# RMS norms of a 512-token block stack: reciprocal root on four columns, spread to rows by TensorE

## The chip, the cores and the metric

The kernel runs on one core of one Trainium2 chip. The metric is the device time of one execution in microseconds. The kernel before took 4485.65 us (median of 3 runs, 4485.53 to 4496.6).

## The reference

Two stacks of transformer blocks work on 512 tokens of width 1024 in fp32. The first has four layers with a mixer (hyena, window attention, pooling, hyena) and a SwiGLU each; the second has one layer with a gated delta rule, latent attention, a merge and an MLP. Ahead of every mixer and every feed-forward stands a root mean square norm:

```python
def rmsnorm(x, g):
    xf = x.astype(jnp.float32)
    y = xf * lax.rsqrt(jnp.mean(xf * xf, axis=-1, keepdims=True) + EPS)
    return (y * g.astype(jnp.float32)).astype(x.dtype)

def _modulate(xn, shift, scale):
    return xn * (1.0 + scale) + shift

# first stack, layer i
h = rmsnorm(x, norm_mix[i]);  x = x + mixer(h)
x = x + swiglu(rmsnorm(x, norm_ffn[i]), ff_w_gate[i], ff_w_up[i], ff_w_down[i])
# second stack
h  = _modulate(_rms(x, norm_attn[l]), mod_x[0], mod_x[1])
hc = _modulate(_rms(ctx, norm_attn[l]), mod_c[0], mod_c[1])
x  = x + mod_x[5] * _sq_relu_mlp(_modulate(_rms(x, norm_mlp[l]), mod_x[3], mod_x[4]), ...)
```

That makes eight norms in the first stack and, in the second, two over the 512 tokens and one over the 256 tokens of the context.

## The kernel before, in words

The activations `x` lie transposed in SBUF: 128 partitions (features) by 8 tiles (`DT`) by 512 tokens (`T`). A sum over the features of a token is therefore a sum over partitions and tiles. Weights come from HBM through a ring of blocks that SyncE loads. Most products (L880 to L882, L891 to L893) are made of three products of rounded high and low parts: ScalarE copies the high part of a weight block (L1748, L1760), GpSimd subtracts it from the block to get the low part (L774, L798), and each product of a 128x128 weight tile with a 128x512 activation tile is three matmuls. PSUM has eight banks: four `acc` banks take the products in rotation and four `aux` banks everything else. Every tile of a rotation is numbered; TensorE waits on `aux_drained[...]` before it writes a bank for the fifth time, and readers wait on `aux_full`.

The order on each engine is that of one list of stages. All synchronisation is by semaphores, and each engine works its queue in order.

A norm goes as follows. ScalarE squares each of the eight tiles of `x` into `xn` (L1764, L1781), VectorE adds squares 1 to 6 onto square 0 (`fold`, L2336), most of it while the stage before still runs. When the last addition is done, TensorE multiplies a 128x128 matrix of ones with the folded tile (L867) and with tile 7 (L870) into one bank. That sums over the partitions and leaves the sum of every token in every partition, as 128x512. Each fp32 matmul is two records in the trace. ScalarE meanwhile loads the table with the square root and makes a dummy root (L1789), then takes the root of the bank into `rstd` (128x512, L1791):

```python
signal(go(rstd, bank(t, aux=True)[:], ACT.Sqrt, bias=eps_col, scale=1.0 / D), root_set)
```

VectorE inverts it in place (L2322 in a norm, L2626 in `modulate`), which also gives the bank free, and makes the eight normed tiles, each a multiplication by the gain of its features and by `rstd` (L2327, L2628):

```python
signal(stt(xn[:, k, :], x[:, k, :], V(gain[0], gain[1] + k), rstd, ALU.mult, ALU.mult),
```

Ahead of a feed-forward or a hyena mixer, ScalarE copies each normed tile to a rounded high part (L1755), VectorE subtracts to get the low part (L2307) and the first products (L891 to L893) run tile by tile as these arrive. Ahead of attention, TensorE waits for all eight tiles (L859). Ahead of pooling, VectorE goes on by itself (L2568 and on). In `modulate` VectorE adds a shift to every tile (L2629). In the first of the two `modulate` stages the norm of the context follows (L1196, L2006, L2641, L2643), in the old form in both kernels. Behind the first norm stands a small product for the attention bias (L1703), and behind a hyena norm the first sine layer (L939).

Elsewhere the kernel has the other form already. The sums over features of q and k heads are columns (L1072, L1281, L1416, L1543: the data is the stationary operand, one column of ones the moving one), their root (L2133) and reciprocal (L2884) are taken on a few columns, and TensorE spreads a column to rows (L1423) with a broadcast column as the stationary operand and the unit matrix as the moving one.

Of the kernel before, what the change touches and what calls it, by code (L numbers as in the profile page):

```python
# [14 lines left out]
P = 128  # L15
T = 512
TC = 256
D = 1024
# [261 lines left out]
def build_program(nc, stream, vecs, tabs, tabs2, x_in, ctx_in, first_mods, scratch, x_keep, diag, solved_t, solved_n, out, schedule):  # L280
# [4 lines left out]
    with ExitStack() as stack:  # L285
# [3 lines left out]
        def sem(name):  # L289
            return stack.enter_context(nc.semaphore(name))  # L290
# [57 lines left out]
        one_col = small_t[:, 7:8]  # L348

# [45 lines left out]
        folded_set = sem("folded_set")  # L395
        root_set = sem("root_set")
# [156 lines left out]
        def _(sp):  # L553
# [43 lines left out]
            def norm(_):  # L597
                n["aux"] += 1
                n["xn"] += DT
# [34 lines left out]
            def modulate(which):  # L634
                n["aux"] += 1 if which else 2
# [78 lines left out]
        def _(pool):  # L714
# [101 lines left out]
            def passes(aux, acc):  # L816
                def stage(_):
# [5 lines left out]
            run({"norm": count(1), "hyena": hyena,  # L823
                 "attention": passes(12 + 16 * 5, 88), "pool": passes(0, DT), "ffn": split("ffn", FT + 2 * DT), "mod": nothing,
                 "modulate": lambda which: n.update(aux=n["aux"] + (1 if which else 2)), "decays": count(2),
# [5 lines left out]
        def _(pe):  # L831
# [31 lines left out]
            def norm(gain):  # L863
                b = open_aux()
                n["fold"] += 1
                pe.wait_ge(folded_set, n["fold"])
                mm(b[:], ones[:], xn[:, 0, :], start=True, stop=False)  # L867
                n["sq"] += DT
                pe.wait_ge(squares_set, n["sq"])
                mm(b[:], ones[:], xn[:, DT - 1, :], start=False, stop=True).then_inc(aux_full, 1)  # L870
                n["xn"] += DT
# [838 lines left out]
        def _(act):  # L1710
# [61 lines left out]
            def norm(gain, then=None):  # L1772
# [17 lines left out]
                t = full(aux, aux_full)  # L1790
                signal(go(rstd, bank(t, aux=True)[:], ACT.Sqrt, bias=eps_col, scale=1.0 / D), root_set)  # L1791
# [482 lines left out]
        def _(dve):  # L2274
# [40 lines left out]
            def norm(gain):  # L2315
                if n["root"] == 0:
                    for k in range(1, DT - 1):
                        fold(k)
                t = aux.take()
                n["root"] += 1  # L2320
                dve.wait_ge(root_set, n["root"])
                drain(nc.vector.reciprocal(rstd, rstd), t, True)  # L2322
                n["xn"] += DT
                target = split_target(gain)
                to = (x_hi_h, xn_r) if target == "hyena" else (x_hi, x_lo)
                for k in range(DT):
                    signal(stt(xn[:, k, :], x[:, k, :], V(gain[0], gain[1] + k), rstd, ALU.mult, ALU.mult),  # L2327
                           plain_set if target else xn_set)
                    if target and k:
                        low(k - 1, *to)  # L2330
                if target:
                    low(DT - 1, *to)

            def fold(k):
                dve.wait_ge(squares_set, n["sq"] + k + 1)
                ins = tt_(xn[:, 0, :], xn[:, 0, :], xn[:, k, :], ALU.add)  # L2336
                if k < DT - 2:
                    step(ins)
                else:
                    signal(ins, folded_set)  # L2340
                    n["sq"] += DT

# [273 lines left out]
            def modulate(which):  # L2616
# [6 lines left out]
                t = aux.take()  # L2623
                n["root"] += 1
                dve.wait_ge(root_set, n["root"])
                drain(nc.vector.reciprocal(rstd, rstd), t, True)  # L2626
                for k in range(DT):
                    step(stt(xn[:, k, :], x[:, k, :], gm[:, 0, k:k + 1], rstd, ALU.mult, ALU.mult))  # L2628
                    signal(ts_(xn[:, k, :], xn[:, k, :], modv[:, shift + k, 0:1], None, ALU.add), plain_set if which else xn_set)  # L2629
                    if which and k:  # L2630
                        low(k - 1)
                if which:
                    low(DT - 1)
# [663 lines left out]
```

## Time and profile before

| | |
|---|---|
| median of 3 runs | 4485.65 us |
| the profiled execution | 4489.94 us |
| its span in the trace | 4488.1 us |
| PE busy | 4152.2 us, 93% |
| DVE busy | 2123.1 us, 47% |
| ACT busy | 1223.2 us, 27% |
| GpSimd busy | 1444.5 us, 32% |
| mean granted TensorE clock | 0.956 of full |

The profiled execution took 1.8 us more than its span, and 4.3 us more than the median of the runs. Times in the views below are microseconds from the start of the span. The granted clock of TensorE has two levels in this trace, 1.00 (2.4 GHz) and 0.50 (1.2 GHz). A fp32 matmul appears as two records of a weight load (PEld) and two of a matmul (PE).

### The profile page before, as it was taken

The numbers are of one execution on the slowest core, as the hardware profiler recorded it, in microseconds if no ns is written. First come the engines' busy times: TensorE is split into PE (matmuls) and PEld (weight loads), VectorE is DVE, ScalarE is ACT, GpSimd is POOL, SyncE is SP. The second block draws the span as 40 slices with busy tenths as digits, with TensorE's granted clock in tenths as the row PEclk, the third lists the DMA queues.
The fourth block names the chain that finished last, engine by engine and source line by source line (L and its number), as shares of the span: only waits on it lengthen the run. The fifth ranks groups of instructions, "written<-read, shape, count | busy, mean of one in ns | idle before, by whom it ended". The sixth has DMA issues, their size and how long they took to land.

```text
span 4488.1 us, 47580 instructions
## 1 busy us (share of the span) xinstructions
PE 4152.2 (93%) x18926; PEld 3071.3 (68%) x18926; DVE 2123.1 (47%) x3109; ACT 1223.2 (27%) x1709; POOL 1444.5 (32%) x834
## 2 busy tenths in 40 slices
PE   7999999899999599989999998979998999998999
PEld 5656788556788378877557886656666665684887
DVE  6567323365413641375763334456664347404322
ACT  3322222134222121233233222322222224422221
POOL 3311344200344144434023442266564000241443
PEclk9999999999999899999999998989999879999999
DMA  6200232210232123221002221221112112221232
GB/s 179 75 18 21 110 102 88 104 47 29 98 114 83 61 97 115 82 78 63 29 29 103 98 95 60 69 57 33 56 34 57 58 67 66 68 98 64 86 104 78
DMA packets 96910, 333.71 MB, mean 74 GB/s; under 512 B 44337, under 2 KB 47537, under 8 KB 67889
## 3 DMA queue, kind: packets, MB, share of 16 engines
q1 hardware_dynamic: 87968, 311.85, 20.5%
q10 hardware_dynamic: 8720, 18.82, 1.7%
q8 instruction: 151, 2.47, 0.2%
q14 instruction: 71, 0.57, 0.0%
HBM read 317.53 MB, written 13.11 MB: 74 GB/s over the span
## 4 chain that ended last, share of the span: by engine, by line
PE 79%; DVE 14%; POOL 2%; ACT 2%; issue 1%; DMA 1%; SPq 0%; DVEq 0%; ACTq 0%; POOLq 0%
PE bank L880 16%; PE bank L881 16%; PE bank L882 16%; PE bank L1314 5%; PE bank L859 5%; PE bank L1082 3%; PE bank L1032 1%; PE bank L1056 1%; PE bank L1612 1%; PE bank L1611 1%; PE bank L1633 1%; PE bank L1543 1%; DVE xn L2327 1%; POOL tab L761 1%; POOL tab L759 1%
## 5 line engine op out<-in xcount | busy, mean ns | idle before, releaser
L774 POOL TENSOR_TENSOR w_lo<-ring,w_hi 128x2048 fp32r<-128x2048 f32 (+2 forms) x200 | 775.3, 3877 | 1532.7 <-ACT w_hi L1748 1532.7
L880 PE MATMUL bank<-x_hi,w_hi 128*128 128x512 f32 x1584 | 618.3, 390 | 9.7 <-POOL w_lo L774 9.7
L881 PE MATMUL bank<-x_lo,w_hi 128*128 128x512 f32 x1584 | 617.0, 389 | 0.0
L882 PE MATMUL bank<-x_hi,w_lo 128*128 128x512 f32 x1584 | 616.9, 389 | 0.0
L1748 ACT ACTIVATE w_hi<-ring 128x2048 fp32r<-128x2048 f32 (+2 forms) x200 | 322.0, 1610 | 866.9 <-PE bank L882 865.9
L880 PE MATMUL bank<-h_hi,w_hi 128*128 128x512 f32 x960 | 373.9, 389 | 0.4
L881 PE MATMUL bank<-h_lo,w_hi 128*128 128x512 f32 x960 | 373.5, 389 | 0.0
L882 PE MATMUL bank<-h_hi,w_lo 128*128 128x512 f32 x960 | 373.4, 389 | 0.0
L880 PEld LDWEIGHTS bank<-x_hi,w_hi 128*128 128x128 f32 x1584 | 297.7, 188 | 73.4 <-POOL w_lo L774 11.8
L882 PEld LDWEIGHTS bank<-x_hi,w_lo 128*128 128x128 f32 x1584 | 297.8, 188 | 61.9
L881 PEld LDWEIGHTS bank<-x_lo,w_hi 128*128 128x128 f32 x1584 | 297.8, 188 | 61.6
L2363 DVE TENSOR_TENSOR xn<-bank,xn 128x512 f32<-128x512 f32 x88 | 60.8, 691 | 589.0 <-PE bank L882 570.0
L1314 PE MATMUL bank<-xn,ring 128*128 128x512 f32 x496 | 240.0, 621 | 1.4 <-DVE work L2671 1.4
L1082 PE MATMUL bank<-work,tab 128*128 128x512 f32 x512 | 228.0, 603 | 12.5 <-ACT work L1886 11.5
L787 POOL TENSOR_TENSOR ring_r<-ring,merge_hi 128x2048 fp32r<-128x2048 f32 x16 | 73.3, 4584 | 506.8 <-ACT merge_hi L2213 506.8
L2353 DVE TENSOR_TENSOR x<-bank,x 128x512 f32<-128x512 f32 x72 | 49.8, 692 | 393.8 <-PE bank L882 347.3
L880 PEld LDWEIGHTS bank<-h_hi,w_hi 128*128 128x128 f32 x960 | 180.2, 188 | 39.3 <-DVE h_lo L2313 2.1
L882 PEld LDWEIGHTS bank<-h_hi,w_lo 128*128 128x128 f32 x960 | 180.2, 188 | 37.4
L881 PEld LDWEIGHTS bank<-h_lo,w_hi 128*128 128x128 f32 x960 | 180.2, 188 | 37.3
L1082 PEld LDWEIGHTS bank<-work,tab 128*128 128x128 f32 x512 | 97.8, 193 | 133.4 <-issue 126.9
L810 POOL TENSOR_TENSOR work<-work,ring 128x1024 f32<-128x1024 f32 x32 | 77.0, 2429 | 266.4 <-ACT work L1855 266.4
L761 POOL TENSOR_TENSOR tab<-tab 56x31 f32<-56x31 f32 (+15 forms) x248 | 150.7, 608 | 19.4
(457 smaller groups left out, 7394.4 us busy)
## 6 DMA issues: line engine op xcount, KB each, us to landing
ring<-stream SPq DMA_DIRECT2D x212, 1024.0 KB, 4.8
ring<-stream SPq DMA_DIRECT2D x64, 704.0 KB, 4.1
ring<-stream SPq DMA_DIRECT2D x36, 512.0 KB, 3.6
xn<-first_mods SPq DMA_DIRECT2D x8, 1024.0 KB, 6.9
ring<-stream SPq DMA_DIRECT2D x4, 1088.0 KB, 5.0
bias_rows<-work ACTq DMA_DIRECT2D x1, 4096.0 KB, 46.3
work<-bias_rows ACTq DMA_DIRECT2D x1, 3072.0 KB, 11.3
tab<-tabs ACTq DMA_DIRECT2D x1, 2624.0 KB, 16.7
```

The costliest lines, as they stand in the source:

```text
L761: solve(tt(W[:, 0:i, i:SUB], W[:, 0:i, i:SUB], part, ALU.subtract))
L774: nc.gpsimd.tensor_tensor(w_lo[:, j % 2, 0:cols], ring[:, k % RING, 0:cols], w_hi[:, j % 2, 0:cols], ALU.subtract).then_inc(wlo_set, 1)
L787: nc.gpsimd.tensor_tensor(ring_r[:, w, 0:2 * DT * P], ring[:, w, 0:2 * DT * P], merge_whi[j % 2][:], ALU.subtract).then_inc(wlo_set, 1)
L810: nc.gpsimd.tensor_tensor(pair, pair, decay[:, pq:pq + 1, :].broadcast_to([P, 2, 512]), ALU.mult).then_inc(filt_set, 1)
L859: ins = mm(b[:], w[:, at + k, :], rhs[k] if isinstance(rhs, list) else rhs[:, k, :], start=(k == 0), stop=(k == kt - 1))
L880: mm(b[:], hi[:, at + k, :], rhs_hi, start=(k == 0), stop=False)
L881: mm(b[:], hi[:, at + k, :], rhs_lo[:, k, :], start=False, stop=False)
L882: ins = mm(b[:], lo[:, at + k, :], rhs_hi, start=False, stop=(k == kt - 1))
L1082: ins = mm(b[:], fwd[kind][:, p, q, ft * P:(ft + 1) * P], source(kind)[:, 2 * p + q, :], start=(q == 0), stop=(q == 1))
L1314: ins = mm(b[:, 0:TC] if ctx else b[:], w[:, at + k, :], src[:, k, :], start=(k == 0), stop=(k == DT - 1))
L1748: signal(go(w_hi[:, j % 2, 0:cols], ring[:, k % RING, 0:cols], ACT.Copy), whi_set)
L2363: drain(tt_(h_tmp[:, f % 2, :], bank(t)[:], gate_tmp[:, f % 2, :], ALU.mult), t)
```

## The change

Ten norms change: the eight `norm` stages and the two norms over 512 tokens of `modulate`. The sum of a token becomes one element of a column: for each chunk of 128 tokens the folded tile is the stationary operand and one column of ones the moving one; the same is done for tile 7 into four more columns. VectorE copies the first four columns to `rstd_col` (128x4) and adds the other four. ScalarE takes the root and VectorE the reciprocal on these 128x4. TensorE then spreads the four columns to a 128x512 bank, and the normed tiles read this bank instead of `rstd`. The bank is given free, by a one-column memset of VectorE, after the eighth normed tile. A norm takes two `aux` tiles instead of one, and the counts of every engine follow. The norm of the context stays.

```diff
@@ PE, norm
-                mm(b[:], ones[:], xn[:, 0, :], start=True, stop=False)
+                for c in range(NB):
+                    mm(b[:, c:c + 1], xn[:, 0, P * c:P * (c + 1)], ones[:, 0:1], start=True, stop=True)
                 n["sq"] += DT
                 pe.wait_ge(squares_set, n["sq"])
-                mm(b[:], ones[:], xn[:, DT - 1, :], start=False, stop=True).then_inc(aux_full, 1)
+                for c in range(NB):
+                    ins = mm(b[:, NB + c:NB + c + 1], xn[:, DT - 1, P * c:P * (c + 1)], ones[:, 0:1], start=True, stop=True)
+                ins.then_inc(aux_full, 1)
+                b = open_aux()
+                pe.wait_ge(rstd_set, n["fold"])
+                for c in range(NB):
+                    ins = mm(b[:, P * c:P * (c + 1)], rstd_col[:, c:c + 1].broadcast_to([P, P]), ident[:], start=True, stop=True)
+                ins.then_inc(aux_full, 1)
@@ ACT, norm
-                t = full(aux, aux_full)
-                signal(go(rstd, bank(t, aux=True)[:], ACT.Sqrt, bias=eps_col, scale=1.0 / D), root_set)
+                t = aux.take()
+                aux.take()
+                act.wait_ge(aux_drained[aux.place(t)], aux.turn(t) + 1)
+                signal(go(rstd_col, rstd_col, ACT.Sqrt, bias=eps_col, scale=1.0 / D), root_set)
@@ DVE, norm (modulate likewise)
-                t = aux.take()
-                n["root"] += 1
-                dve.wait_ge(root_set, n["root"])
-                drain(nc.vector.reciprocal(rstd, rstd), t, True)
+                t, rows = rstd_rows()
...
-                    signal(stt(xn[:, k, :], x[:, k, :], V(gain[0], gain[1] + k), rstd, ALU.mult, ALU.mult),
+                    signal(stt(xn[:, k, :], x[:, k, :], V(gain[0], gain[1] + k), rows, ALU.mult, ALU.mult),
                            plain_set if target else xn_set)
                     if target and k:
                         low(k - 1, *to)
+                rows_read(t)
                 if target:
                     low(DT - 1, *to)
@@ DVE, new
+            def rstd_rows():
+                t = full(aux, aux_full)
+                b = bank(t, True)
+                step(nc.vector.tensor_copy(rstd_col, b[:, 0:NB]))
+                ins = tt_(rstd_col, b[:, NB:2 * NB], rstd_col, ALU.add)
+                drain(ins, t, True)
+                n["root"] += 1
+                dve.wait_ge(root_set, n["root"])
+                signal(nc.vector.reciprocal(rstd_col, rstd_col), rstd_set)
+                t = full(aux, aux_full)
+                return t, bank(t, True)[:]
+
+            def rows_read(t):
+                which = aux_drained[t % BANKS]
+                nc.vector.memset(small_t[:, 25:26], 0.0).then_inc(which, 1)
+                dve.wait_ge(which, t // BANKS + 1)
```

## Rows read from the trace of the kernel before

**Rows 1.** The page: busy time (share of span) and instructions; the chain by engine.
```profile
PE 4152.2 (93%) x18926; PEld 3071.3 (68%) x18926; DVE 2123.1 (47%) x3109; ACT 1223.2 (27%) x1709; POOL 1444.5 (32%) x834
...
PE 79%; DVE 14%; POOL 2%; ACT 2%; issue 1%; DMA 1%; SPq 0%; DVEq 0%; ACTq 0%; POOLq 0%
```

**Rows 2.** The chain in order of time, around one norm: start, length, what.
```profile
472.98 0.70 DVE xn L2336
473.81 1.10 PE bank L867 x2
474.91 0.87 PE bank L870 x2
475.87 0.70 ACT rstd_t L1791
476.66 3.37 DVE rstd_t L2322
480.05 0.76 DVE xn L2327
...
482.46 0.77 PE bank L891
```

**Rows 3.** VectorE's instructions on `rstd_t`: duration ns min/median/max, first and last start.
```profile
L2327 DVE SCALAR_TENSOR_TENSOR xn<-x,vec,rstd_t x64: 750/752/3577, 23.7 to 2411.7; 128x512 f32<-128x512 f32 x64
...
L2322 DVE RECIPROCAL rstd_t<-rstd_t x8: 3352/3354/3355, 20.3 to 2398.5; 128x512 f32<-128x512 f32 x8
...
L2626 DVE RECIPROCAL rstd_t<-rstd_t x2: 3352/3352/3353, 2781.2 to 4108.5; 128x512 f32<-128x512 f32 x2
```

**Rows 4.** Timeline from 195: column sums at full clock and their reader.
```profile
194.86 3.63 PE L1072 MATMUL bank<-ones,work 128*128 128x1 f32 x32
...
198.62 0.18 DVE L2420 RECIPROCAL small_t<-bank 128x4 f32<-128x4 f32 x1 [2.22 <-PE bank L1072]
```

**Rows 5.** Timeline from 3506: column sums, root, reciprocal, spread, reader of the bank.
```profile
3506.43 1.16 PE L1423 MATMUL bank<-ident,tab 128*128 128x128 f32 x8 [0.15 <-DVE tab L2884]
...
3510.19 1.22 PE L1416 MATMUL bank<-ones,work 128*128 128x1 f32 x8 [1.71 <-ACT work L2078]
3511.51 0.27 ACT L2133 ACTIVATE tab<-bank,small_t 128x4 f32<-128x4 f32 x1 [1.46 <-PE bank L1416]
3511.88 0.18 DVE L2884 RECIPROCAL tab<-tab 128x4 f32<-128x4 f32 x1 [1.04 <-ACT tab L2133]
...
3512.11 2.07 PE L1423 MATMUL bank<-ident,tab 128*128 128x128 f32 x8 [0.70 <-DVE tab L2884]
3514.29 0.75 DVE L2901 SCALAR_TENSOR_TENSOR work<-work,vec,bank 128x512 f32<-128x512 f32 x1 [2.23 <-PE bank L1423]
```

**Rows 6.** Stretches: length, PE, PEld, DVE, ACT, POOL busy, granted clock, DMA.
```profile
475.77:482.46 6.69, 0.00 (x0) 0.03 (x1) 5.66 (x5) 1.95 (x3) 0.00 (x0) 0.80 0.07 29
482.46:486.67 4.21, 4.21 (x10) 3.34 (x11) 4.04 (x6) 1.72 (x3) 0.00 (x0) 0.50 0.00 0
...
3616.70:3620.10 3.40, 3.40 (x33) 3.40 (x32) 0.00 (x0) 0.00 (x0) 0.00 (x0) 1.00 0.95 393
3620.10:3623.50 3.40, 3.40 (x13) 2.87 (x14) 0.61 (x3) 0.22 (x1) 0.00 (x0) 0.50 0.49 205
```

**Rows 7.** Timeline from 3446: column sums at half clock.
```profile
3446.05 2.70 PE L1281 MATMUL bank<-tab,work 128*128 128x1 f32 x12
```

**Rows 8.** Timeline of the first norm: GpSimd's subtraction and the normed tiles.
```profile
22.19 4.50 POOL L798 TENSOR_TENSOR ring_r<-ring,z_lo 128x2048 fp32r<-128x2048 f32 x1 [20.57 <-ACT z_lo L1760]
23.66 4.36 DVE L2327 SCALAR_TENSOR_TENSOR xn<-x,vec,rstd_t 128x512 f32<-128x512 f32 x2
```

**Rows 9.** Timeline of the first `modulate`: last fold and first normed tile.
```profile
2775.71 0.69 DVE L2336 TENSOR_TENSOR xn<-xn 128x512 f32<-128x512 f32 x1 [7.52 <-ACT xn L1764]
...
2784.57 0.75 DVE L2628 SCALAR_TENSOR_TENSOR xn<-x,gm,rstd_t 128x512 f32<-128x512 f32 x1
```

**Rows 10.** The page's costliest groups: an addition that reads a bank.
```profile
L2353 DVE TENSOR_TENSOR x<-bank,x 128x512 f32<-128x512 f32 x72 | 49.8, 692 | 393.8 <-PE bank L882 347.3
```

More of the change, by code:

```diff
@@ L348, in build_program @@
         one_col = small_t[:, 7:8]
+        rstd_col = small_t[:, 28:32]
         def carve(*sizes):
@@ L395, in build_program @@
         folded_set = sem("folded_set")
+        rstd_set = sem("rstd_set")
         root_set = sem("root_set")
@@ L597, in norm @@
             def norm(_):
-                n["aux"] += 1
+                n["aux"] += 2
                 n["xn"] += DT
@@ L634, in modulate @@
             def modulate(which):
-                n["aux"] += 1 if which else 2
+                n["aux"] += 2 if which else 3
             def decays(_):
@@ L822, in _ @@
             nothing = count(0)
-            run({"norm": count(1), "hyena": hyena,
+            run({"norm": count(2), "hyena": hyena,
                  "attention": passes(12 + 16 * 5, 88), "pool": passes(0, DT), "ffn": split("ffn", FT + 2 * DT), "mod": nothing,
-                 "modulate": lambda which: n.update(aux=n["aux"] + (1 if which else 2)), "decays": count(2),
+                 "modulate": lambda which: n.update(aux=n["aux"] + (2 if which else 3)), "decays": count(2),
                  "gdn": gdn, "mla": nothing, "merge": merge,
@@ L2622, in modulate @@
                     step(tt_(gm[:, c, :], gm[:, c, :], gain, ALU.mult))
[L2623 to L2626, printed above, removed]
+                t, rows = rstd_rows()
                 for k in range(DT):
-                    step(stt(xn[:, k, :], x[:, k, :], gm[:, 0, k:k + 1], rstd, ALU.mult, ALU.mult))
+                    step(stt(xn[:, k, :], x[:, k, :], gm[:, 0, k:k + 1], rows, ALU.mult, ALU.mult))
                     signal(ts_(xn[:, k, :], xn[:, k, :], modv[:, shift + k, 0:1], None, ALU.add), plain_set if which else xn_set)
@@ L2631, in modulate @@
                         low(k - 1)
+                rows_read(t)
                 if which:
```

## The prediction

> **What bounds the kernel now.** I read the page's busy times and its chain first: TensorE is busy 93% of the span and carries 79% of the chain, VectorE 14% [rows 1]. So the kernel is a stream of matmuls, and what a norm costs is the time in which that stream stands still. The chain in order of time shows it for the norm behind the first hyena mixer [rows 2]: the last fold ends at 473.68 (472.98 + 0.70), the sums run from 473.81, the root from 475.87, the reciprocal from 476.66 and the first normed tile from 480.05; the first product starts at 482.46. From the end of the fold to the first normed tile it is 6.37 us, and more than half of it is the 128x512 reciprocal, 3.37 us. Everything in this stretch is on the chain; TensorE does nothing from 475.77 to 482.46 [rows 6]. The same reciprocal stands in all ten norms, x8 and x2, each 3352 to 3355 ns [rows 3]. I read the other norms' timelines too: eight of the ten have this pattern within 0.02 us. The two others are the first norm, which runs beside a GpSimd subtraction [rows 8], and the first `modulate`, which starts at half clock and takes 8.17 us from the end of the fold (2775.71 + 0.69 = 2776.40) to the first tile at 2784.57 [rows 9].
>
> The change therefore touches ten stretches of the chain, about 66 us together, 1.5% of the time, and nothing else of weight.
>
> **The change part by part, for one of the eight.**
>
> - Fold to sums: 473.68 to 473.81, 0.13 us, stays [rows 2].
> - Column sums. Before, four records of 512 columns, from 473.81 until the root starts at 475.87: 2.06 us. Now there are 8 fp32 matmuls of one column, 16 records, each behind its own weight load. At full clock 32 such records take 3.63 us (0.113 each), and their reader starts 3.76 us after the first [rows 4]; 16 of them then take 3.76 - 16 x 0.113 = 1.95 us. At half clock 12 take 2.70 us, 0.225 each [rows 7]; 16 take 3.60 us and, with the 0.13 us to the reader, 3.73 us. These are the ends.
> - Copy and addition on 128x4: new. The nearest row is a 128x4 operation of VectorE that reads a bank, 0.18 us [rows 4]; two of them, 0.03 us between them and 0.06 us to ScalarE make 0.45 us.
> - Root on 128x4 instead of 128x512: 3511.51 to 3511.88, 0.37 us with the hand-over to VectorE, where the row before had 0.79 us (475.87 to 476.66) [rows 5, 2].
> - Reciprocal on 128x4: 3511.88 to 3512.11, 0.23 us with the hand-over to TensorE, where 3.39 us stood (476.66 to 480.05) [rows 5, 2].
> - The spread: four fp32 matmuls, 8 records of 128 columns. The kernel has just this elsewhere: 2.07 us at half clock, its reader starting 2.18 us after the first record, and 1.16 us at full clock, which with the same 0.11 us gives 1.27 us [rows 5].
>
> With everything at full clock the chain is 0.13 + 1.95 + 0.45 + 0.37 + 0.23 + 1.27 = 4.40 us, 1.97 less than now. With everything at half clock it is 0.13 + 3.73 + 0.45 + 0.37 + 0.23 + 2.18 = 7.09 us, 0.72 more than now. So the reciprocal's 3.1 us are there to be had, and the clock decides how many of them TensorE takes back.
>
> What the trace says of the clock: in 3616.70 to 3620.10 TensorE is busy the whole time with one-column sums (33 records) at 1.00, and in the next stretch it runs at 0.50 (1.2 GHz) [rows 6]. The sums in rows 7 run at 0.50 behind a like train. And the spread at 3506.43 takes 1.16 us while the one at 3512.11, behind 8 one-column sums (1.22 us), takes 2.07 us [rows 5]. So the clock falls behind one-column sums in which TensorE counts as busy. Before, the two 512-column sums run at full clock, TensorE then idles 6.69 us, over which the mean clock is 0.80, and the first ten records of product run at 0.50 for 4.21 us [rows 6]. After the change the wide sums are gone, and the last wide work is the products of the stage before. I expect the fall within the few us behind that: about as often in the column sums as behind them, and nearly always before the spread, which starts some 3.5 us after the fold. I take 2.4 us for the sums (between 1.95 and 3.73; nearer to the full-clock row, as the fall, where it comes in them, leaves only their second part slow) and 2.18 us for the spread (the half-clock row). That gives 0.13 + 2.4 + 0.45 + 0.37 + 0.23 + 2.18 = 5.76 us, 0.61 less than now. Eight norms: 4.9 us.
>
> The half-clock stretch of the products behind stays: they still start 2.41 us behind the first tile (480.05 to 482.46), with TensorE idle before them [rows 2]. It starts earlier by what the norm saves, no more.
>
> - First `modulate`: it starts at half clock, so 8.17 us become 7.09: 1.1 us saved. The context sums queued behind the spread on TensorE move back some 2 us; their reader, ScalarE's second root, waits for the last normed tile more than 9 us later, which hides it.
> - First norm: also at half clock. The first normed tile starts 7.09 us behind the fold's end at 15.70, at 22.79 instead of 23.66. There is a second thing. That tile should take 0.75 us, but the first two take 4.36 us together while GpSimd's subtraction runs from 22.19 to 26.69 [rows 8], and the largest of the 64 is 3577 ns against a median of 752 [rows 3]. So VectorE's operation with two SBUF inputs was held until GpSimd was done. With the rows in a bank it has one SBUF input. I take it to go through; but the subtraction for the low part of tile 0 (two SBUF inputs) is held in its place, to about 27.35 (GpSimd's end, 0.1 later than before, and the 0.55 us that the held one took behind it), where it ended at 28.75 before. Saved: 1.4 us. If the tile is held as before, it is nothing to 0.9.
> - The memset that frees the bank: VectorE's small operation and its wait, 0.1 us, in front of the last low part. Seven times it hides behind TensorE, which is late there after its half-clock stretch; ahead of pooling it is on the chain. I take 0.1 us in all, at most 1.
> - Waits added: ScalarE waits for VectorE's addition instead of for TensorE. Behind it stand the copies of high parts, which need normed tiles anyhow. TensorE waits for the reciprocal; behind it stand the bias product and the sine layer (about 1 us each), which fit in the 5 us before the first product. No DMA and no SyncE step moves; the second `aux` tile per norm is free long before its bank comes round.
>
> Sum: 4.9 + 1.1 + 1.4 - 0.1 = 7.3 us. The profiled execution would go from 4489.94 to 4482.6 us. It lies 4.3 us above the median of the runs; from the median 4485.65 I get 4478.
>
> A page speaks against the multiplications. The Trainium skill, "VectorE: DVE Perf Modes", section "The TRN2 errata — SBUF-src ops pay a fixed extra latency per instruction", gives VectorE a fixed term of 120 cycles with a PSUM source and 58 with SBUF, at 0.96 GHz 65 ns more; over 80 normed tiles an estimate of 5.2 us by that page, and 4483 instead of 4478. The trace disagrees: a multiplication that reads a bank takes 0.75 us [rows 5] against 752 ns from SBUF [rows 3], and an addition 692 ns from a bank [rows 10] against 0.69 [rows 9]. I count nothing.
>
> A page bears on the first norm: the Trainium skill, "SBUF — State Buffer", section "SBUF: two separate sides", says that a VectorE operation with two SBUF inputs contends with a GpSimd operation that reads SBUF, and the later one waits for the other's end. By that rule the bank input goes through (1.4 us), without it 0.9 at most; rows 8 agree with it as far as the old form goes.
>
> **The rivals.**
>
> - *The clock holds through sums and spread.* 1.97 x 8 = 15.8 us, with 2.4 us of the two others 18 us: 4467. For it: the fall has been seen only behind trains of one-column sums, and here they are short. Against: rows 5, where eight of them sufficed. If the clock also held into the products, up to 4.21 - 10 x 0.23 = 1.9 us more in seven norms, 4455.
> - *The other side: the clock falls ahead of the sums.* If losing the wide sums lets it fall before the column sums begin, each of the eight costs 0.72 us more than now: +5.8 - 1.1 - 1.4 + 0.1 = +3.4, 4489. It decides where the sums take more than 2.4 + 7.3 / 8 = 3.3 us on average. For it: half clock at the start of the first `modulate`, behind 9 us of idling. Against: the gap here is under 2 us behind dense products, and the wide sums before started at full clock.
> - *Reading the bank is dearer than SBUF*: the 4483 above on the page's terms; from rows, 0.
>
> **How the numbers follow.** Forecast 0.56, clock holds 0.15 (and into the products 0.05), clock falls early 0.18, the dearer bank or something else 0.06. About 0.3% (13.5 us) is what a measurement of this kernel can tell from no change; the forecast's 7.3 us lie within it. The forecast's own range is 4472 to 4484; the range to 4463 and 4491 takes in the two neighbouring cases. Faster by over 0.3% (below 4472.2): 0.2 from the two cases with the held clock and 0.02 of the forecast's edge. Slower by over 0.3% (above 4499.1): no case reaches it, 0.04 for what I have not seen. Within: 0.74.
>
> **What would show it.** The reciprocals fall from 33.5 us to about 2. Column sums between 1.9 and 3.8 us per norm, differing from norm to norm by where the clock falls; spreads mostly at 2.07 and seldom at 1.16. First normed tile about 5.8 us behind the fold's end instead of 6.37. No 3577 ns tile in the first norm. I am wrong if spreads at full clock are the rule, if the fall comes before the sums, or if normed tiles take clearly over 0.75 us.

## The result, and the profile after

The changed kernel takes 4497.35 us (median of 20 runs, 4489.35 to 4501.64), the kernel before took 4488.61 in the same session (20 runs, 4479.96 to 4499.58). The ratio is 1.0018, 95% interval 1.0011 to 1.0025: the change costs 5 to 11 us where I forecast a gain of 7, and 4497.35 lies above the range given (4463 to 4491). The profiled execution took 4501.48 us (span 4499.7), against 4489.94 before.

The page after; the lines answer to [rows 1]:
```profile
PE 4197.2 (93%) x19126; PEld 3120.5 (69%) x19126; DVE 2100.6 (47%) x3139; ACT 1219.3 (27%) x1709; POOL 1444.8 (32%) x834
...
PE 79%; DVE 13%; POOL 3%; ACT 2%; issue 2%; DMA 1%; SPq 0%; DVEq 0%; ACTq 0%; POOLq 0%
```
VectorE has lost 22.5 us of work, which is what was wanted. TensorE is busy 45 us longer with 200 more matmuls. The norms explain the 200 records (ten times 16 + 8 - 4), but only 22 of the 45 us (their sums and spreads keep TensorE busy for 44.7 us in all, the wide sums did for 22.9); the rest must be old matmuls that got slower.

The norm behind the first hyena mixer, where [rows 2] stood. Chain in order of time: start, length, what.
```profile
477.71 0.70 DVE xn L2346
...
478.55 1.02 PE bank L870 x8
479.58 0.91 PE bank L874 x8
...
480.57 0.17 DVE small_t L2356
480.77 0.17 DVE small_t L2357
...
481.03 0.30 ACT small_t L1803
...
481.42 0.19 DVE small_t L2361
...
481.75 2.06 PE bank L879 x8
...
483.90 0.76 DVE xn L2336
...
486.32 0.76 PE bank L901
```
From the fold's end (478.41) to the first normed tile it is 5.49 us instead of 6.37, and from there to the first product (486.32) 2.42, as before (2.41). So the norm itself is 0.88 us shorter. The same stretches by busy time, granted clock in the eighth column, as in [rows 6]:
```profile
478.55:480.98 2.43, 1.92 (x16) 1.83 (x16) 0.32 (x2) 1.36 (x2) 0.00 (x0) 1.00 0.89 378
480.99:481.75 0.76, 0.00 (x1) 0.03 (x1) 0.18 (x1) 0.30 (x1) 0.00 (x0) 0.50 0.01 0
481.75:483.81 2.06, 2.05 (x8) 1.75 (x8) 0.00 (x0) 0.00 (x0) 0.00 (x0) 0.50 0.00 0
...
486.32:491.23 4.91, 4.91 (x12) 3.84 (x13) 4.70 (x7) 1.89 (x3) 0.00 (x0) 0.50 0.01 3
491.23:495.00 3.77, 3.77 (x18) 3.13 (x17) 3.60 (x6) 1.68 (x3) 0.00 (x0) 1.00 0.00 0
```
The clock falls at 480.98, 2.57 us behind the fold (before it fell 6.17 us behind it in this norm, and 4.4 to 6.6 us in the eight norms that lie alike), so the spread runs at half clock. And the products now spend 4.91 us at half clock, where they spent 4.21.

The small operations, answering to [rows 3]: duration in ns, min/median/max.
```profile
L2356 DVE COPY small_t<-bank x10: 160/161/163, 19.8 to 4119.1; 128x4 f32<-128x4 f32 x10
L2357 DVE TENSOR_TENSOR small_t<-bank,small_t x10: 160/161/163, 20.0 to 4119.3; 128x4 f32<-128x4 f32 x10
L2361 DVE RECIPROCAL small_t<-small_t x10: 177/178/179, 20.6 to 4119.9; 128x4 f32<-128x4 f32 x10
```
The normed tiles that read the bank:
```profile
L2336 DVE SCALAR_TENSOR_TENSOR xn<-x,vec,bank x64: 746/748/749, 23.1 to 2422.4; 128x512 f32<-128x512 f32 x64
```
No tile of 3577 ns is left. The spread, by its records:
```profile
L879 PE MATMUL bank<-ident,small_t x80: 421/421/580, 20.9 to 4121.9; 128*128 128x128 f32 x80
```
All 80 have a half-clock duration (at full clock eight of them take 1.16 us in all [rows 5]). The timeline of the first norm, where [rows 8] stood:
```profile
22.55 4.51 POOL L800 TENSOR_TENSOR ring_r<-ring,z_lo 128x2048 fp32r<-128x2048 f32 x1 [20.93 <-ACT z_lo L1770]
...
23.05 1.53 DVE L2336 SCALAR_TENSOR_TENSOR xn<-x,vec,bank 128x512 f32<-128x512 f32 x2 [2.24 <-PE bank L879]
...
24.63 2.98 DVE L2319 TENSOR_TENSOR xn_r<-xn,x_hi_h 128x512 fp32r<-128x512 f32 x1
```
Two normed tiles now go through beside GpSimd, and the next operation with two SBUF inputs is held to 27.61, GpSimd's end and 0.55 us, in their place.

**Norm by norm.** From the fold's end to the first normed tile, before and after: 6.38 and 5.50 us in five norms (three of the four ahead of an ffn, the one ahead of the second hyena mixer, the second `modulate`), 6.38 and 5.70 in two (ahead of attention and of pooling), 6.38 and 6.81 in one (ahead of the ffn behind pooling), 8.17 and 7.13 in the first `modulate`, 7.96 and 7.07 in the first norm. Together 7.3 us saved. All this is one execution: in a second trace of the same kernel (the first experiment) nine of the ten norms are within 0.1 us of this, and the norm ahead of the ffn behind pooling takes 5.06 us instead of 6.81.

**Where the time went.** I cut both traces at the ends of the folds and compare the stages, each with the norm at its head:

| stage | before us | after us | after less before |
|---|---|---|---|
| first hyena mixer | 457.97 | 462.42 | +4.45 |
| ffn 0 | 373.49 | 372.93 | -0.56 |
| attention | 282.42 | 282.37 | -0.05 |
| ffn 1 | 373.25 | 373.00 | -0.25 |
| pooling | 66.07 | 66.07 | 0.00 |
| ffn 2 | 376.24 | 376.66 | +0.42 |
| second hyena mixer | 450.32 | 457.59 | +7.27 |
| ffn 3 | 380.94 | 380.52 | -0.42 |
| second stack | 1329.10 | 1329.39 | +0.29 |
| last mlp | 382.64 | 382.76 | +0.12 |

Two readings. No stage gets all that its norm saves: pooling gets none of 0.68, attention 0.05 of 0.68, ffn 0, 1 and 3 get 0.25 to 0.56 of 0.88, the last mlp none. And one stage, the second hyena mixer, loses 7.3 us although its norm saves 0.88. (The first hyena mixer's stage differs from one execution of the same kernel to the next by more than that, 452.9 to 462.4 in two of the changed kernel; I set it aside.) Behind the first product of the second hyena mixer, first before and then after: the stretch from the first product to the rise of the clock, the whole stage behind it, and 30 us in its middle (not quite the same work: 112 matmul records and 99).
```profile
1953.93:1957.81 3.88, 3.87 (x9) 3.14 (x10) 3.71 (x6) 1.38 (x3) 0.00 (x0) 0.50 0.00 0
1953.93:2395.47 441.54, 412.64 (x1540) 283.36 (x1540) 297.97 (x336) 135.58 (x170) 117.55 (x33) 0.96 0.14 48
2163.00:2193.00 30.00, 28.09 (x112) 18.38 (x112) 17.03 (x21) 9.00 (x15) 7.32 (x4) 0.94 0.00 1
```
```profile
1957.33:1962.37 5.04, 5.04 (x12) 3.97 (x13) 4.83 (x7) 1.89 (x3) 0.00 (x0) 0.50 0.00 0
1957.33:2407.01 449.68, 421.30 (x1540) 289.70 (x1540) 300.06 (x337) 135.57 (x170) 117.61 (x33) 0.95 0.13 47
2169.00:2199.00 30.00, 29.65 (x99) 19.06 (x100) 15.97 (x20) 6.84 (x12) 5.07 (x3) 0.83 0.00 1
```
The same 1540 matmuls, the same work on ScalarE and GpSimd, but TensorE busy 8.7 us longer and the stage 8.14 us longer. Counting through the stage with its norm, TensorE stands at half clock for 34.1 us before and 54.6 after, and half of the 20.5 us between them is 10, near the 8 that are lost: the products did not change, the clock falls under them more often. Aligning the 1540 records of the two traces one by one, the distance between them grows by 8.7 us inside stretches that are at half clock in one of the traces, and shrinks by 0.6 us outside them.

### The profile page after: what moved, and what is told of

It reads as the page before. It is cut to its first block, busy times and chain, and to the rows that moved or that the text cites. A ratio compares the mean times of both kernels' runs of the same rounds, so it can differ in the third digit from the quotient of the medians.

```text
span 4499.7 us, 48040 instructions
## 1 busy us (share of the span) xinstructions
PE 4197.2 (93%) x19126; PEld 3120.5 (69%) x19126; DVE 2100.6 (47%) x3139; ACT 1219.3 (27%) x1709; POOL 1444.8 (32%) x834
## 4 chain that ended last, share of the span: by engine, by line
PE 79%; DVE 13%; POOL 3%; ACT 2%; issue 2%; DMA 1%; SPq 0%; DVEq 0%; ACTq 0%; POOLq 0%
PE bank L890 16%; PE bank L891 16%; PE bank L892 16%; PE bank L1324 5%; PE bank L861 5%; PE bank L1092 3%; PE bank L1042 2%; PE bank L1066 2%; PE bank L1622 1%; PE bank L1621 1%; PE bank L1643 1%; PE bank L1553 1%; POOL tab L763 1%; DVE xn L2336 1%; POOL tab L761 1%
## 5 line engine op out<-in xcount | busy, mean ns | idle before, releaser
L1042 PE MATMUL bank<-tab,work 128*128 128x256 f32 x512 | 128.3, 414 | 30.8 <-DVE work L2524 30.8
```

The costliest lines, as they stand in the source:

```text
L1042: ins = mm(b[:, 256 * p:256 * (p + 1)], U[:, 4 * ft + 2 * kind + p, ct * P:(ct + 1) * P], inv[kind][:, p, ft, :], start=(j == 0), stop=(j ...
```

## The experiments

The theory: the half-clock stretch behind a norm ends at an instant that the clock sets and not the kernel. Work of fixed length follows, so each norm fixes how the stage behind it lies to the clock's further instants. The change moves that, and the second hyena mixer meets them badly. (The expectations below call this the phase theory: the phase is where the work lies between two such instants.) The main rivals: the added bank turns, the column sums or the narrow root as such cost time further on; the difference is scatter; the fall ahead of the spread is the whole loss. Ratios are to the kernel before on the same chip, with 95% intervals, and times are medians.

**The changed kernel again** (no edit).

> The changed kernel once more, for a second trace. Phase theory (the instants at which the clock falls stand in a fixed relation to the work, because each stretch at half clock ends at such an instant and the work behind it is of fixed length): the falls behind the feed-forward norms come again 2.5 to 2.7 us behind the end of the fold, as in five norms of the first trace, and the hyena stages again hold clearly more than the 34 us at half clock that the second hyena stage of the kernel before had. Chance theory (each execution draws its own phase): both numbers scatter by more than 1 us from norm to norm and execution to execution, and the hyena stages are as often short as long. Time 4492 to 4502 us by both.

4497.17 us, ratio 1.0012 (1.0002 to 1.0023); profiled execution 4492.14. The first hyena mixer's stage is 452.89 here, and from there to the end it is 4021.5 us, as in the first trace (4021.3), against 4014.4 before. The second hyena mixer's stage is 457.64 again, so its 7.3 us are the kernel's, not scatter. The falls ahead of ffn 0, 1 and 3 come 2.5 to 2.8 us behind the fold, about as the phase theory has it. The one ahead of the ffn behind pooling does not come again: it stood 0.49 us behind the fold in the first trace and stands 3.83 us behind it here, within the spread, whose eight records take 1.61 us, between the 1.16 of full and the 2.05 of half clock:
```profile
1566.72 1.61 PE L879 MATMUL bank<-ident,small_t 128*128 128x128 f32 x8 [1.28 <-DVE small_t L2361]
```
That norm is 1.75 us shorter than in the first trace, 5.06 instead of 6.81, and its stage is 376.54 instead of 376.66. One kernel thus shows by itself that what a norm saves can be gone by the end of its stage.

**The old arithmetic on the new banks.** Wide sums, root and reciprocal as before; two `aux` tiles a norm, the second filled by a single one-column matmul and freed by the memset.
```diff
-                for c in range(NB):
-                    mm(b[:, c:c + 1], xn[:, 0, P * c:P * (c + 1)], ones[:, 0:1], start=True, stop=True)
+                mm(b[:], ones[:], xn[:, 0, :], start=True, stop=False)
...
                 b = open_aux()
-                pe.wait_ge(rstd_set, n["fold"])
-                for c in range(NB):
-                    ins = mm(b[:, P * c:P * (c + 1)], rstd_col[:, c:c + 1].broadcast_to([P, P]), ident[:], start=True, stop=True)
-                ins.then_inc(aux_full, 1)
+                mm(b[:, 0:1], ones[:], ones[:, 0:1], start=True, stop=True).then_inc(aux_full, 1)
```

> The sums, root and reciprocal on 128x512 as before, but two aux tiles per norm, the second written by a one-column matmul and freed by the memset: the bank rotation, the waits and the memset of the change alone. Bank theory (the shifted rotation makes waits in the hyena stages): the hyena stages lose their 5 to 8 us each here too, 4498 to 4506 us. Phase theory: nothing moves by more than 0.1 us in a norm, so the time is that of the kernel before, within 3 us. Column theory (what costs is that the wide sums are gone): also that of the kernel before.

4490.85 us, 1.0003 (0.9992 to 1.0013). The second hyena mixer's stage is 450.30, behind the first product 441.51: the kernel before's. Bank turns, memsets and their waits are cleared. Further on this trace shows what does scatter: the second stack takes 1325.17 us where the kernel before had 1329.10, the last mlp 381.00 where it had 382.64. Differences of up to 4 us in the second stack are therefore not read as effects here.

**Delays in the two hyena norms.** Memsets of the now unused `rstd_t` ahead of the small reciprocal, two and then four of them; one took 0.65 us.
```diff
+                for _ in range(delay):
+                    step(nc.vector.memset(rstd_t[:], 0.0))
                 signal(nc.vector.reciprocal(rstd_col, rstd_col), rstd_set)
```

> The changed kernel with two VectorE memsets of 128x512 (about 1.0 us together) ahead of the small reciprocal in the two norms before hyena mixers only. Phase theory: the hyena stages meet the clock's instants elsewhere, and the time moves by much more or by another sign than the 2 us put in: at least 4 us away from the changed kernel plus 2 here or in the 2 us variant. Bank theory and every theory by which an instruction or a wait costs: the changed kernel plus 2 us, within 1.5.

> The same with four memsets (about 2.1 us). Phase theory: as in the 1 us variant; of the two, one is expected to have stretches at half clock as few as in the kernel before (34 us in a hyena stage), and to be faster than the changed kernel in spite of the delay. Theories of cost: the changed kernel plus 4 us, within 1.5.

Two memsets: 4484.59 us, 0.9985 (0.9973 to 0.9998). Four: 4484.82, 0.9993 (0.9982 to 1.0003), an interval that takes in no difference from the kernel before. Both medians lie 12 us below the changed kernel's 4497.17 on the same chip. In both the first normed tile comes later by the memsets' 1.3 and 2.6 us, and the second hyena mixer's stage is shorter all the same: 450.88 and 447.82, where the changed kernel had 457.6. Added work on the chain that shortens its stage by 6.7 and 9.8 us is what the theory says and no rival does.

**One memset, in the norm ahead of the second hyena mixer alone.**
```diff
+                t, rows = rstd_rows(1 if gain == ("norm_mix", 3 * DT) else 0)
```

> The changed kernel with one VectorE memset (0.65 us in the chain, as measured in the delayed kernels) in the norm ahead of the second hyena mixer only. Phase theory: the distance from the stage's first product to the rise of the clock behind it is 5.04 us in the changed kernel (stage behind the first product 449.7 us), 3.88 in the kernel before (441.5) and 4.10 with 1.3 us of delay (441.7). Here it becomes about 4.4, on the side of the good ones: 442 us behind the first product if the step lies above 4.4, 449.7 if below; the kernel 3 to 7 us faster than the changed one (4490 to 4494) or no faster. Theories of cost: 0.65 us slower than the changed kernel.

4481.77 us, 0.9981 (0.9971 to 0.9991). The stage takes 447.12 us. One memset of 0.65 us in a chain of 4.5 ms takes 10.5 us off its stage and turns a kernel that is slower than before into one that is faster. The direction is the one that the phase theory gave; the size is not: 442 or 449.7 us were expected behind the first product, and it is 438.56, and the whole is faster than the 4490 to 4494 that were expected. The theory says that the stage changes with its phase, not by how much. First product to rise of the clock, and the stage behind the first product:
```profile
1957.75:1962.06 4.31, 4.31 (x10) 3.44 (x11) 4.14 (x6) 1.82 (x3) 0.00 (x0) 0.50 0.00 0
1957.75:2396.31 438.56, 409.76 (x1540) 282.35 (x1540) 299.61 (x337) 135.52 (x170) 117.47 (x33) 0.97 0.13 49
```
The same 1540 matmuls as above, now at a mean clock of 0.97.

**The loss made in the kernel before.** No part of the change; memsets of an unused buffer ahead of its wide reciprocal in that norm, 2.2 us in all, chosen to bring the distance from first product to rise to the changed kernel's.
```diff
+                if gain == ("norm_mix", 3 * DT):
+                    for w in (512, 512, 512, 128):
+                        step(nc.vector.memset(kbuf2[:, 0:w], 0.0))
                 drain(nc.vector.reciprocal(rstd, rstd), t, True)
```

> The kernel before with four memsets (2.2 us) ahead of the reciprocal in the norm before the second hyena mixer only. Nothing of the change is in it. Phase theory: the first product moves 2.2 us nearer to the rise of the clock that followed it by 3.88 us, too near to count, and the next rise then stands about 5.1 us behind it, as in the changed kernel: the stage behind the first product takes 449 to 450 us instead of 441.5, and the kernel is about 10 us slower than before (4498). Theories of cost: 2.2 us slower (4490).

4495.86 us, 1.0011 (1.0002 to 1.0021). The stage takes 460.72 instead of 450.32: 2.2 us of delay and 8.2 behind it. (By the ratio the whole is 1 to 9 us slower than before, where about 10 were expected.)
```profile
1953.61:1958.66 5.05, 5.05 (x12) 3.99 (x13) 4.84 (x7) 1.89 (x3) 0.00 (x0) 0.50 0.00 2
1953.61:2403.31 449.70, 421.34 (x1540) 290.12 (x1540) 297.50 (x336) 135.51 (x170) 117.56 (x33) 0.95 0.13 47
```
449.70 us, where the changed kernel has 449.68. With all runs beside one another in which the products start at half clock, equal distances give equal stages, whichever norm is in front. It is no matter of longer or shorter: the longest distance has the shortest stage.

| kernel | first product to rise us | stage behind first product us |
|---|---|---|
| old arithmetic on the new banks | 3.82 | 441.51 |
| before | 3.88 | 441.54 |
| changed, two memsets | 4.10 | 441.66 |
| changed, one memset | 4.31 | 438.56 |
| changed, one memset, filled attention norm | 4.50 | 438.53 |
| changed | 5.04 | 449.68 |
| before, delayed 2.2 us | 5.05 | 449.70 |
| changed, again | 5.08 | 449.73 |
| changed, four memsets | 6.05 | 437.27 |

**The kernel before with TensorE kept busy in the norms.** Matmuls that nobody reads, into the next `acc` bank, behind the wide sums of seven norms.
```diff
+            def fill(*widths):
+                t = acc.n
+                if t >= BANKS:
+                    pe.wait_ge(acc_drained[acc.place(t)], acc.turn(t))
+                for w in widths:
+                    mm(bank(t)[:, 0:w], ones[:], vec[:, 0:w], start=True, stop=True)
...
+                elif gain[0] == "norm_ffn":
+                    fill(*[512] * 7, 256)
+                elif gain[1] == 3 * DT:
+                    fill(*[512] * 6)
+                elif gain[1] == DT:
+                    fill(*[512] * 12)
```
The last norm has `fill(*[512] * 8)`.

> The kernel before with matmuls that nobody reads (ones with the first columns of the vectors, into the acc bank that the next product overwrites) behind the sums of seven norms, 6.0 to 7 us each (12 fp32 matmuls, 10 us, ahead of attention). Phase and clock theory: the clock stays at full through the norm and the products start at full clock; each of the six norms with split products saves 4.2 us of half clock, worth up to 1.9 us and at least 0.5 (VectorE's pace of 1.5 us per tile then bounds): 3 to 11 us in the stages of the feed-forwards together, the hyena stage to be seen (its falls are later and elsewhere). If the clock in these stretches is of no account: 0, or slower by what the fillers delay.

4479.15 us, 0.9978 (0.9968 to 0.9987): the fastest of all that ran, though its interval overlaps those of the one memset, and its 4479.15 lies 11 us below the kernel before's 4490.26 on the same chip. Its norm behind the first hyena mixer, TensorE alone: eleven of the fill's records and the first products.
```profile
477.60 4.46 PE L868 MATMUL bank<-vec,ones 128*128 128x512 f32 x11
482.31 0.47 PE L908 MATMUL bank<-x_hi,w_hi 128*128 128x512 f32 x1 [0.25 <-DVE x_lo L2324]
482.62 0.40 PE L909 MATMUL bank<-x_lo,w_hi 128*128 128x512 f32 x1
```
The first product takes 0.47 us instead of 0.77 [rows 2], and no filled norm shows the half clock. The norm's own chain is unchanged, and still ffn 0, 1 and 3 are 0.9 to 1.1 us shorter, attention 2.7 and the second hyena mixer 4.0. (The ffn behind pooling is 1.6 us longer and pooling 0.7; why is open.) Over the seven filled stages it comes to 8.4 us, near the 7.3 us that the change takes off the norms; not all of it is the half clock behind the norm, since the phase of the second hyena mixer moved too.

**The changed kernel, kept busy.** Can one have both: the short chain and the clock? Fills ahead of the sums, ahead of the spread and behind it.
```diff
+                if held:
+                    fill(512)
                 pe.wait_ge(folded_set, n["fold"])
...
+                if held:
+                    fill(512, 128)
                 pe.wait_ge(rstd_set, n["fold"])
```

> The changed kernel with such matmuls ahead of the column sums (0.85 us), between sums and spread (1.07 us) and behind the spread (1 to 6 us) in eight norms. Clock theory: spread at full clock (1.2 instead of 2.05 us), first normed tile 4.5 to 4.7 us behind the fold, products at full clock: 1 us and up to 2 us more in each norm against the changed kernel, and against the filled kernel before 1.7 to 1.9 us in each, 10 to 14 us; 4475 or less. If the column sums still make the clock fall, the first normed tile stays at 5.5 us and the filled changed kernel is no faster than the unfilled one.

4487.38 us, 0.9984 (0.9971 to 0.9997), with runs from 4464.31 to 4497.8; 4475 or less was expected of a held clock. The clock held in two norms, ahead of ffn 0 and ffn 2. TensorE in the former: sums, fill, spread, fill, first product.
```profile
475.73 1.05 PE L881 MATMUL bank<-ones,xn 128*128 128x1 f32 x8 [0.78 <-DVE xn L2369]
476.64 1.03 PE L885 MATMUL bank<-ones,xn 128*128 128x1 f32 x8
477.53 1.33 PE L870 MATMUL bank<-vec,ones 128*128 128x512 f32 x4
478.86 1.16 PE L892 MATMUL bank<-ident,small_t 128*128 128x128 f32 x8
479.86 2.31 PE L870 MATMUL bank<-vec,ones 128*128 128x512 f32 x6
482.54 0.47 PE L924 MATMUL bank<-x_hi,w_hi 128*128 128x512 f32 x1 [0.36 <-DVE x_lo L2342]
```
With the clock held the spread takes 1.16 us and the chain 4.46; the stage is 370.47 us, 1.92 less than the 372.39 of the filled kernel before, and 1.92 is just the difference of the chains (6.38 less 4.46). With the products at full clock a shorter chain reaches the end of its stage: ffn 1 has a chain of 5.76 and is 0.63 us shorter than the filled kernel before's (6.38 less 5.76 is 0.62). In the other six filled norms the clock fell 1.9 to 2.7 us behind the fold all the same, with chains of 5.37 to 5.85.

It had risen again before the products came, and this separates two things: whether the products start at half clock, and how the stage lies to the clock. Ahead of the second hyena mixer it rose 1.69 us before the first product:
```profile
1948.79:1953.83 5.04, 5.04 (x22) 3.64 (x22) 4.83 (x7) 1.90 (x3) 0.00 (x0) 1.00 0.00 0
1948.79:2398.59 449.80, 422.23 (x1543) 289.35 (x1542) 297.86 (x337) 135.54 (x170) 117.56 (x33) 0.95 0.13 47
```
The first 5 us run at full clock, and the stage behind the first product is still the long one, 449.80 us. In the next run the clock rose 2.92 us before the first product, and the stage behind it is the kernel before's, 441.57. The half-clock products at its head are not what makes the stage long.

**More fill.** Wider ahead of the sums and of the spread, and a piece between the two halves of the sums.
```diff
-                    fill(512)
+                    fill(512, 256)
...
+                if held:
+                    fill(256)
...
-                    fill(512, 128)
+                    fill(512, 256)
```

> The filled changed kernel with more unread matmuls: 1.28 us ahead of the column sums instead of 0.85, 0.43 us between their two halves, 1.28 us before the spread instead of 1.07. In the filled kernel the clock still fell 1.9 to 2.7 us behind the fold in five of eight norms. Theory that the column trains make it fall: it now holds in all eight, the first normed tile comes 4.9 us behind the fold in each (4.46 plus 0.43) and no norm lies above 5.2; the feed-forward stages take 371 to 372 us. The hyena stages are no longer tied to the clock's instants by the norm ahead of them and may be long or short, so the time of single executions scatters over 20 us or more; median 4470 to 4484. If the clock falls for another reason, norms at 5.4 to 5.9 us remain.

4480.7 us, 0.9984 (0.9975 to 0.9993), within the 4470 to 4484 expected, but not by the way expected, which was a clock held in all eight norms. It held in three (ahead of ffn 1, pooling and ffn 2), with chains of 4.90, and fell in five, 2.4 to 2.9 us behind the fold, with chains of 6.40 to 6.50. That the trains of one-column sums alone bring the fall is not confirmed: cutting them did not hold the clock. What else it is, is open.

**One memset, and the norm ahead of attention filled** (`fill(*[512] * 6)` behind its spread).
```diff
+                if gain == ("norm_mix", DT):
+                    fill(*[512] * 6)
...
+                t, rows = rstd_rows(1 if gain == ("norm_mix", 3 * DT) else 0)
```

> The changed kernel with the 0.65 us delay ahead of the second hyena mixer and 5 us of unread matmuls behind the spread of the norm ahead of attention only, to see whether the two gains add. Behind the filled norm of the kernel before the attention stage took 279.7 us instead of 282.4. Phase theory: attention 279.5 to 280.5, the second hyena stage again 447 us, since the feed-forward norms between them tie the work to the clock's instants again; 2 to 3 us faster than with the delay alone, 4479. If the tie is not restored, the second hyena stage takes 450 us or more and the gain is lost.

4481.19 us, 0.9983 (0.9975 to 0.9992). Attention takes 279.30 us instead of 282.4 and the second hyena mixer 447.09, both as expected, but the whole is no faster than with the memset alone (0.9981). In the two profiled executions the second stack's stage, 1329.6 us here and 1326.4 there, took back the 3.1 us that attention gave; it scatters by as much between runs without an edit near it, so whether the gains add is not shown.

## Why the prediction was wrong

**The norms did what their steps said.** For one of the eight I forecast 5.76 us from the fold to the first tile, and the mean of the eight is 5.71. Of the terms only one is off by more than 0.1. The column sums take 2.02 us to their reader in five norms, 2.23 in two and 3.34 in one, on average 2.24 and not 2.4: in five of the eight the clock falls behind them, in two it falls near their end (ahead of attention and of pooling), and in one, ahead of the ffn behind pooling, near their start. Halves of its sums:
```profile
1572.91 1.52 PE L870 MATMUL bank<-ones,xn 128*128 128x1 f32 x8 [1.73 <-DVE xn L2346]
1574.30 1.84 PE L874 MATMUL bank<-ones,xn 128*128 128x1 f32 x8
```
There it is 6.81 us, near the 7.09 worked out for half clock throughout. The reciprocal with its hand-over takes 0.33, not 0.23. Copy and addition 0.46 (0.45), root 0.39 (0.37) and spread 2.15 (2.18) stand. The spread at half clock in all ten norms stands too, the first `modulate` (7.13 against 7.09), and the first norm: its first product comes 1.43 us earlier, forecast 1.4, through the mechanism given, the hold handed on to the low part. To their first tiles the norms saved 7.3 us; with the first norm taken at its first product, as the forecast did, it is 7.8, forecast 7.3. (The stretches add up to 67 us, not 66; nothing hangs on it.) The mean of 5.71 owes something to chance: one norm of 6.81 stands in it, and in the second trace, where that norm takes 5.06, the mean is 5.50.

**The step that failed** is the sentence "The half-clock stretch of the products behind stays [...] It starts earlier by what the norm saves, no more", and with it the claim that the change touches ten stretches "and nothing else of weight". The stretch starts earlier, but its end does not come earlier: 8.79 + 3.88 = 12.67 us behind the fold before the second hyena mixer, 7.91 + 5.04 = 12.95 after, and within 0.5 us of where it was in ffn 0, 1 and 3 and the last mlp. So the saved 0.88 us is spent at half clock, and half of it is given back at once. In pooling all of it is: VectorE bounds that stage almost to its end, its last 16 matmuls start 0.68 us earlier behind the fold (55.06 instead of 55.74), and the clock's rise under them comes 0.70 later (59.73 instead of 59.03).
```profile
1558.58 8.74 PE L859 MATMUL bank<-work,ring 128*128 128x512 f32 x16 [19.00 <-DVE x L2349]
```
```profile
1561.76 9.42 PE L861 MATMUL bank<-work,ring 128*128 128x512 f32 x16 [20.70 <-DVE x L2376]
```
From the seventh matmul on they stand where they stood, 60.03 us behind the fold, and the stage takes 66.07 us in both traces. Attention fits neither account: there the first rise comes 3.0 us earlier (15.36 instead of 18.39) and the stage still gets 0.05 us, with 23.9 us at half clock in all in both traces; a later stretch took the difference. All this alone would have left a small gain: the other eight stages from ffn 0 to the end show -0.5 us together. What turned the sign is that the clock's later falls lie differently under the second hyena mixer: +8.1 us in its stage. The runs show this on both sides, by undoing it in the changed kernel with one memset (-10.5 us) and by making it in the kernel before with a delay (+8.2 us beside the delay itself).

**The rivals.** The clock did not hold through the whole spread anywhere in the changed kernel (through half of it once, in the second trace); its price was right, 4.46 us where I worked out 4.40, and the filled kernel shows it in two norms. The fall did not come ahead of the sums, though in one norm it came 0.49 us behind the fold, soon after they began. The bank is not dearer: the normed tile takes 748 ns from a bank against 752 from SBUF. So the surcharge of the Trainium skill, "VectorE: DVE Perf Modes", section "The TRN2 errata — SBUF-src ops pay a fixed extra latency per instruction", by which a PSUM source would cost 65 ns more, is not there for this operation. The rule of the Trainium skill, "SBUF — State Buffer", section "SBUF: two separate sides", held in both directions: the tile with one SBUF input passed beside GpSimd in 0.75 us, the next operation with two was held for 2.98 us. The rival that came true is one that I had not named: that a norm's length sets the phase of what follows.

**What stays open.** Which features of the second hyena mixer make a distance of 5.04 us bad and 4.31 good; I have the relation in nine traces of the table and two more with the clock up at the first product, not its cause record by record. Why the filled column-sum norms lose the clock in some places and keep it in others. What moves the first hyena mixer's stage where nothing in it differs (462.4, 452.9, 462.5 and 453.2 us in the four traces with the changed kernel's first stage); that its lie to the clock's instants at launch does so would fit, but was not tested.

## What to carry to other kernels

In this kernel, bound by TensorE, a stall of some microseconds costs the stall and a half-clock stretch behind it, and the end of that stretch mostly did not come earlier when the stall got shorter. So a saving of less than a microsecond per stall can be given back whole, and the total can move by ten microseconds in either direction through work that was not touched: cut the trace into stages, compare them and their granted clocks one by one, and try the change with a small delay or two before judging it. Where TensorE would idle anyway, unread matmuls in the gap were worth more here (0.9978) than the shorter arithmetic (1.0018), and with them in place a shorter chain did reach the end of its stage.

## What I had not expected of the hardware

- A delay of 0.65 us made one stage 10.5 us shorter, and one of 2.2 us made the same stage of the other kernel 10.4 us longer, of which 2.2 is the delay.
- Stages are repeatable to a few hundredths of a microsecond once a norm has fixed how they lie to the clock: 449.68, 449.73 and 449.70 us over two kernels, 66.06 to 66.08 us for pooling in nine executions.
- In the changed kernel the clock fell 0.5 to 2.7 us behind the fold in every one of the eight norms (1.6 to 3.8 in the second trace), behind or within column sums that kept TensorE busy for 1.9 us in five of them; behind two 512-column sums it fell at 4.4 to 6.6 us.
